# Where two maxima over partitions and a set of output scales are computed in a two-layer hybrid encoder

## The reference

```
mod = silu(c) @ w_ada + b_ada;  shift, scale, gate = split(mod)
h = rms_norm(x, g_norm) * (1 + scale) + shift
q_lat, kv_lat, k_rope, z_a, q_b, k_b, v_b, z_b = split(h @ w_in)
a: 8 heads over low-rank queries and keys (rank 256 and 128), rotary part shared
b: 8 query heads over 2 key heads, each row normalised, 2-D rotary
x = x + gate * (concat(attn_a * silu(z_a), attn_b * silu(z_b)) @ w_out)
```

## Time and profile before

| | us |
|---|---|
| median of 3 runs (lowest, highest) | 2351.36 (2350.35, 2354.43) |
| the profiled execution's own time | 2351.27 |
| its span, first to last instruction | 2349.2 |
| PE busy | 2143.6 (91%) |
| DVE busy | 1504.2 (64%) |
| ACT busy | 985.9 (42%) |
| POOL busy | 812.1 (35%) |

### The profile page before, as it was taken

One profiled execution on the slowest core, in us unless ns is written; L12 is line 12 of the kernel. 1 busy time (PEld: TensorE's weight loads), 2 busy tenths in 40 slices (PEclk: granted clock), 3 DMA queues, 4 the chain that ended last, 5 costly groups with the idle time before them and its releaser, 6 DMA issues.

```text
span 2349.2 us, 41398 instructions
## 1 busy us (share of the span) xinstructions
PE 2143.6 (91%) x16698; PEld 1311.8 (56%) x16698; DVE 1504.2 (64%) x2490; ACT 985.9 (42%) x2190; POOL 812.1 (35%) x1343
## 2 busy tenths in 40 slices
PE   4889998897999999999989999989799999999997
PEld 1445554455666666666645555545466666666664
DVE  3567665576766666666745665648686666666664
ACT  1133344224654445444522434523365444544542
POOL 0563331575331233123036533139443123123210
PEclk8999999899999999999999999999999999999998
DMA  8812234530100000000442011366020100010001
GB/s 289 318 46 73 72 126 165 195 146 37 55 25 14 28 19 10 28 19 13 145 147 90 19 37 54 112 216 222 10 81 11 37 28 13 35 37 23 15 28 46
DMA packets 80153, 181.04 MB, mean 77 GB/s; under 512 B 8192, under 2 KB 34886, under 8 KB 79962
## 3 DMA queue, kind: packets, MB, share of 16 engines
q1 hardware_dynamic: 79964, 178.39, 21.4%
HBM read 130.11 MB, written 39.88 MB: 72 GB/s over the span
## 4 chain that ended last, share of the span: by engine, by line
PE 69%; DVE 23%; ACT 3%; issue 2%; DMA 2%; SPq 1%; POOL 0%; DVEq 0%; POOLq 0%; ACTq 0%
PE psum L694 33%; PE psum L676 10%; PE psum L685 7%; PE psum L687 7%; PE psum L686 7%; DVE nmax L1263 5%; PE psum L914 5%; DVE hT L1018 2%; DVE PT_next L1280 2%; DVE region L1280 2%; ACT region L1475 1%; DVE region L1215 1%; ACT region L1459 1%; DVE region L1240 1%; DVE region L1289 1%
## 5 line engine op out<-in xcount | busy, mean ns | idle before, releaser
L676 PE MATMUL psum<-ident,region 128*128 128x128 f32 (+2 forms) x3224 | 445.7, 278 | 54.8 <-DVE PT_next L1280 14.5
L676 PEld LDWEIGHTS psum<-ident,region 128*128 128x128 f32 (+2 forms) x3224 | 361.1, 141 | 120.8 <-issue 59.6
L1263 DVE TENSOR_REDUCE nmax<-psum 128x1 f32<-128x1024 f32 (+1 forms) x384 | 398.3, 1037 | 18.6 <-PE psum L694 17.8
L1483 ACT ACTIVATE region<-psum 128x512 f16<-128x512 f32 x384 | 214.6, 592 | 307.8 <-PE psum L676 307.0
L1280 DVE TENSOR_TENSOR region<-psum,region 128x512 f16<-128x512 f32 x384 | 251.5, 682 | 142.6 <-ACT region L1483 142.3
L694 PE MATMUL psum<-KTa,region 96*128 96x512 f32 x640 | 309.5, 599 | 5.4 <-DVE region L1224 5.3
L1538 POOL TENSOR_TENSOR region<-region,rope_sb 128x64 f32<-128x64 f32 (+3 forms) x384 | 162.3, 444 | 305.6 <-DVE region L1220 295.6
L1483 ACT ACTIVATE PT_next<-psum 128x512 f16<-128x512 f32 x256 | 138.9, 594 | 271.2 <-PE psum L676 271.2
L1475 ACT ACTIVATE region<-psum,nmax,unscale 128x1024 f32<-128x1024 f32 (+1 forms) x192 | 204.5, 1065 | 107.4 <-DVE nmax L1266 106.7
L1475 ACT ACTIVATE region<-psum,nmax 128x1024 f32<-128x1024 f32 (+1 forms) x192 | 186.9, 974 | 140.9 <-DVE nmax L1263 140.7
L694 PE MATMUL psum<-Wq,hT 128*128 128x512 f32 (+1 forms) x512 | 202.9, 543 | 2.1 <-DVE region L1226 2.1
(11 more groups left out here) (171 smaller groups left out, 3398.3 us busy)
## 6 DMA issues: line engine op xcount, KB each, us to landing
w_in_parts<-parts SPq DMA_DIRECT2D x28, 512.0 KB, 2.9
Wq<-w_in_parts SPq DMA_DIRECT2D x16, 896.0 KB, 7.0
Wq<-in_w_in SPq DMA_DIRECT2D x6, 2048.0 KB, 15.1
Va<-in_w_ada SPq DMA_DIRECT2D x12, 1024.0 KB, 5.6
hT<-h_transposed SPq DMA_DIRECT2D x24, 512.0 KB, 3.3
Wout<-in_w_out SPq DMA_DIRECT2D x4, 2048.0 KB, 11.9
h_transposed<-parts SPq DMA_DIRECT2D x16, 512.0 KB, 2.9
Wout<-in_w_out SPq DMA_DIRECT2D x16, 512.0 KB, 4.7
```

Source lines behind the costliest of these rows:

```text
L676: return nc.tensor.transpose(out, in_, ident[0:n, 0:n])
L1263: last = nc.vector.reduce_max(nmax[:, h:h + 1], scores_buf(h, S), AX_X, negate=True)
L1483: nc.scalar.activation(pt(h, S, 0, 4 * c)[:, 0:4, :], psum[:, T_BANK + b, :].rearrange("p (c n) -> p c n", c=4), ACT.Copy).then_inc(s["pt_ ...
```

## The change

There are three edits, on POOL and DVE alone.

- POOL, start of the program: the root of the second tile's rows of instance 0 is worked out right behind that of the first, ahead of the wait for the local maxima and the maximum over partitions. The later instances keep their call where it was.
- POOL, instance 1: the maximum over partitions for layer 1's modulation, with its wait, goes from the head of the instance to tile 2, slot 0.
- DVE, instances 1 and 3: `output_scales()` is called at the end of key step NT - 1, ahead of the two drain steps, and no longer in slot 0 of the first tile.

```
                     if r and (not isinstance(i, int) or i + 1 < NT):
                         h_low(i + 1, 1 - odd)
+                    if r and i == NT - 1:
+                        output_scales()
...
                         else:
-                            if first and h == 0:
-                                output_scales()
                             if first:
                                 output_weights(h)
...
             x_rstd(0)
+            x_rstd(1)
             pool.wait_ge(s["maxima_local"], 1)
...
-                if q == 1:
-
-                    pool.wait_ge(s["maxima_local"], 2)
-                    nc.gpsimd.partition_all_reduce(maxima[:, 6:8], maxima[:, 6:8], P, RMAX).then_inc(s["maxima_ready"], 1)
-                x_rstd(b0 + 1)
+                if q:
+                    x_rstd(b0 + 1)
                 pool.wait_ge(s["wukv_loaded"], 16 * (q + 1))
...
                         for name in names:
                             at[name] = rounds.step()
+                        if q == 1 and (i, h) == (W_SCALE_TILE, 0):
+                            pool.wait_ge(s["maxima_local"], 2)
+                            nc.gpsimd.partition_all_reduce(maxima[:, 6:8], maxima[:, 6:8], P, RMAX).then_inc(s["maxima_ready"], 1)
                         if r == 0 and (i, h) == (W_SCALE_TILE, 0):
```

## The result

Before, on the same chip: 2350.86 us median of 4 runs (2346.82 to 2354.43). After: **2318.80 us** (2313.82 to 2321.70, 4 runs), a ratio of 0.9862 with a 95% interval of 0.9838 to 0.9886. The profiled execution of the changed kernel took 2318.16 us (span 2316.1, mean granted clock 0.987 against 0.977), 33.1 us less than the profiled one of before. The forecast was 2318.2. Sequence 0 to 3 are here the four instances q = 0 to 3.

What follows compares the result with a forecast made beforehand. TensorE led the chain (69%), so gains had to come where PE stands: behind two POOL maxima and DVE's output scales. 7.7 + 8.8 + 16.6 = 33.1 us off 2351.3 gives 2318.2; own range 2315 to 2322, wider range 2312 to 2327.

Steps and rivals of the forecast that it cites:

- A: Start of sequence 0: root ahead of the maximum, second key product 6.68 us earlier and 1.02 faster; 7.7 us, 6.7 to 8.8.
- B: Start of sequence 1: layer 1's maximum gone, second key product 7.0 us earlier and 1.8 faster; 8.8 us, 7.0 to 9.6.
- C: First tile of sequences 1 and 3: scales moved, 6.3 us stall plus 2.0 clock each; 16.6 in all, 12.4 to 17.0.
- the template: Start of the third sequence, without a maximum: 4.93 us from first key eviction to second product, which then takes 7.56.
- The cover of A: Start of sequence 0: third rows ready near 61, PE ends the second product at 61.5, so POOL's hold stays hidden.
- The bound of A: Start of sequence 0: gain not above about 8.8 us, since PE at full clock, ready at 59.8, would wait for POOL.
- The moved maximum: Tile 2 of sequence 1: costs POOL up to 15.6 us, in 40.11 us of idle time, so nothing.
- The second rival: Tile 2 of sequence 1: the next instruction pays the hold, gates 9.4 us late; gain 23.7, time 2327.6; chance 0.04.
- one slow head: First tile of sequence 1: head after the stall took 5.46 us at clock 0.60, 3.45 at full clock; gain 2.0.
- The first: Rival at the starts: POOL's hold to 54.70 makes third rows late; about 2 us instead of 7.7, time 2323.9; chance 0.10.
- The third: Rival at the key starts: something else holds the second rows, only the scales' 16.6 us remains, time 2334.7; chance 0.04.
- The fourth: Rival at the end of the key phase: moved scales wait for the gate row from DRAM; slower, 2356 us; chance 0.02.

Runs made afterwards that it cites:

- C alone: Kernel before with only the output scales moved to the end of the key steps: 2334.67 us, ratio 0.9936.
- B alone: Kernel before with only layer 1's maximum moved to tile 2 of sequence 1: 2342.03 us, ratio 0.9965.
- The experiment: Kernel before, scales left in the first tile, POOL's gate product with Wout held until they are done: 2332.56 us, ratio 0.9939.
- the next version: Changed kernel with the second tile's transposes and modulation ahead of the first key product in each sequence: 2311.13 us, ratio 0.9851; again 2311.42, 0.9838.
- A and B alone: Kernel before with one edit each: second rows' root ahead of the first maximum, 2340.40 us; layer 1's maximum moved to tile 2, 2342.03 us.

## Why the prediction was right, and where its terms were off

The forecast was 33.1 us less and a profiled time of 2318.2; it came to 33.1 and 2318.16. The mechanism was right in all three parts. That the sum came out to the tenth is luck: A and B were each about 1 us too high, C was 0.5 too low, and 1.6 us (1.75 + 1.3 - 1.4) came at places that no step spoke of. The changed kernel gained 32.1 us between the medians of one chip and 28.7 on the other, which is how far the match can be trusted.

- **The places.** Right, all three. The eviction 4.93 us ahead of the second product as the template says: 49.15 to 54.08. The chain has no POOL step left at the first key steps.
- **A, 7.7 predicted, 6.5 to 6.7 measured.** The start was right (53.95; 54.08). The term that was mis-sized is the product behind it: 7.56 was taken from sequence 2, it took 8.60. The windows view of the changed kernel has a difference between the two places. In sequence 0 the granted clock is 0.68 over the first product, ahead of the gap, and 0.68 over the second; in sequence 2 the first product took 5.75, at a granted clock of 1.00:

```profile
40.60:49.10 8.50, 8.50 (x18) 4.48 (x19) 5.43 (x12) 0.00 (x0) 0.40 (x1) 0.68 0.98 361
54.08:62.68 8.60, 8.60 (x18) 4.49 (x19) 0.00 (x0) 1.15 (x1) 7.28 (x20) 0.68 0.91 309
66.62:72.40 5.78, 5.78 (x17) 3.18 (x18) 2.36 (x6) 1.15 (x1) 5.16 (x17) 1.00 1.05 396
421.10:428.60 7.50, 7.50 (x18) 3.92 (x19) 1.28 (x1) 3.31 (x4) 4.98 (x17) 0.77 0.75 310
```

- **What that shows and what not.** The four traces with the root early and the old order of the key step have 8.37 to 8.60 us for this product. In sequence 2, after the same gap of 4.10, the product took 7.55 in seven traces and 8.26 in two (C alone, the maximum behind the root). So the template's own price moves between executions by most of the term's error. That the low clock ahead of the gap makes it dearer fits the rows; no run varied it alone.
- **The cover of A.** Right, and close. The third rows' root came at 58.41 (59.3 at the latest was said), PE waited for DVE alone at the third product (66.62). The runs with the second tile first show that the cover was thin: there the hold became the bound.
- **The bound of A.** Its upper end (8.8) leaves out the root itself; with rows "ready near 61", as the prediction has it, the same working gives 8.2. Nothing hung on it.
- **B, 8.8 predicted, 7.85 measured, 9.54 in the repeat.** The start was right: 3.71 us from eviction to product (417.39 to 421.10; 3.7 said). The product is the term that missed: after a gap of 2.87 us it took 7.55, the slower of the two times whose middle I took. But that is no fixed price of this gap. In the repeat of the changed kernel the same product took 5.85 us after the same gap:

```profile
423.59 5.85 PE L694 MATMUL psum<-region,hT 128*128 128x416 f32 x16 [2.87 <-DVE hT L1018]
```

There the low clock lay earlier, over the 32 out products (15.47 us, 14.00 in the first trace), and the start of sequence 1 had come only 5.79 us earlier, not 8.28. So both prices that the prediction named occur with one and the same kernel (7.55 in its first trace, with B alone and with the maximum behind the root; 5.85 in its second).
- **The moved maximum.** Right: 6.23 us ahead of it and no delay behind it. The second rival, a hold that the next instruction pays whatever the idle time, is refuted: POOL's gates come 26.26 us earlier than before (738.09 to 711.83), as the rest of the tile does, and 0.09 us behind ACT, as before. That the cost is one hold for a run of maxima is shown by the two in a row.
- **C, 16.6 predicted, about 17.1 measured** (10.1 and 6.9), 15.2 alone. Both mechanism and new place were right. The scales take 2.91 us there; the eviction behind them comes 1.0 us late against PE's work (495.85, where 510.96 less 16.13 would be 494.83), as said, and the next 0.1, with nobody waiting. Of the 8.3 for each place, 6.3 were the stall and 2.0 the clock. Over the stall itself the traces have 8.54 and 8.36, so this term was right to 0.3 us at each, and the rest of C's miss lies elsewhere. I had priced one slow head and not the one at 574.75, whose 1.7 us came on top.
- **The contention.** The Trainium skill (GPSIMD Engine Reference, "Key points") says that POOL and VectorE share their SBUF interfaces and contend where VectorE has two inputs in SBUF. The experiment agrees: 2.27 us with POOL's pieces beside it, 0.16 without. Of the length of the wait, here to the end of the piece of 2.3 us that POOL is at, that section says nothing.
- **The other rivals.** The first (POOL bounds the starts) was wrong for the change and became right in the first sequence of the next version. The third fell with A and B alone. The fourth fell with the scales following the instruction before them without idle, at 492.94. But the transfers didn't all move up with PE's steps, as the prediction has it: PE waits 1.0 us longer for one at 152.18.

## What to carry to other kernels

Where an engine is held behind a special operation, look at what is queued behind it in program order, and put the one instruction with a waiter ahead of it. Where a small operation takes the time of somebody else's large one, move either of the two; here the one gave 8.5 us at its place and the other 7.2. When a stall goes, count the clock that it took with it, but give that term a range: look at the same product in several traces before taking its time from one place, as equal gaps were followed by 5.85 and 7.55 us, and by 7.55 and 8.26.

## What the runs showed of the hardware

- **The hold behind a maximum over partitions.** In sequence 0 it took 8.57 to 11.36 us in twelve traces of twelve executions (8.57, 8.97, 9.33, 9.44, 9.53, 9.59, 9.81, 10.13, 10.20, 10.58, 11.35, 11.36), and 6.96 to 7.86 at the start of sequence 1, in the six kernels that have a maximum there. It was paid once for two in a row. What POOL does in it, and why the first is longer and wanders, is open; no run tried it. The Trainium skill (GPSIMD Engine Reference, "2.1 Instruction dispatch") names some 6 us ahead of the first call of newly loaded code, in which no instruction is seen; the 5.82 and 6.23 us ahead of a maximum are of that length, though no trace shows what they are. It does not speak of the time behind.
- **Two-input operations of VectorE on 128 x 1 values** took 0.16 us with POOL idle, 0.16 to 0.40 beside its short pieces at the end of the key phase, and 1.29, 2.07 and 2.27 us while POOL multiplied pieces of 2.3 us. Those with one input stayed at 0.15 to 0.21.
- **One kernel's time moves between runs by as much as an edit gives.** Medians of the kernel before differed by 2.5 us between the chips, its single runs went from 2340.88 to 2354.43, and in one trace 3.9 us came between two sequences with no edit near (two maxima in a row: 1.1 us ahead of before at the start of sequence 2, 5.0 at that of sequence 3).
